# A new order of loads and products at the start of a two-block transformer kernel, and nine modulation rows moved from the attention to the projection before it

## What is computed

```python
def first_block(x, c, ...):                      # x: 512 rows of 1024
    mod = silu(c) @ w_ada + b_ada                # 3072 numbers
    shift, scale, gate = split(mod, 3)
    h = rms_norm(x, norm_pre) * (1 + scale) + shift
    proj = h @ w_in                              # 1024 -> 3072 columns
    xa, ga, q, k, v, gb = split(proj, 512 columns each)
    ya = rms_norm(rg_lru(conv(xa)) * silu(ga))   # gated linear recurrence over the rows
    yb = rms_norm(attention(rotary(q), rotary(k), v) * silu(gb))   # 8 heads of 64
    return x + gate * rms_norm(concat(ya, yb) @ w_out, norm_post)

def second_block(x, c_2, ctx_2, ...):
    mod = silu(c_2) @ w_ada_2 + b_ada_2          # 6144 numbers, and again for the context
    ...                                          # differential attention, RWKV scan, mixture of experts
```

## Time and profile before

| | us |
|---|---|
| median of 3 runs | 1869.47 |
| lowest and highest | 1867.77, 1876.37 |
| the profiled execution | 1878.58 |
| its span in the trace | 1876.8 |

### The profile page before, as it was taken

One profiled execution on the slowest core, in us unless ns is written; L12 is line 12 of the kernel. 1 busy time (PEld: TensorE's weight loads), 2 busy tenths in 40 slices (PEclk: granted clock), 3 DMA queues, 4 the chain that ended last, 5 costly groups with the idle time before them and its releaser, 6 DMA issues.

```text
span 1876.8 us, 37887 instructions
## 1 busy us (share of the span) xinstructions
PE 1717.6 (92%) x16822; PEld 927.4 (49%) x16822; DVE 804.7 (43%) x1484; ACT 518.8 (28%) x983; POOL 109.4 (6%) x144
## 2 busy tenths in 40 slices
PE   5999999999999999999999999999999977778786
PEld 3444566544546555556667667544454333323332
DVE  3853144656627456355654554344462211222210
ACT  3710254311127422354453341122231110101010
POOL 0000010010000000100000000000001101010100
PEclk8999989999989999999998998899999999999998
DMA  9121376351110030042221210356569999999997
GB/s 396 76 88 47 145 287 247 145 224 69 45 45 1 23 151 0 17 170 82 77 81 50 63 56 24 114 219 221 219 239 398 416 425 415 422 413 425 417 423 279
DMA packets 48360, 359.25 MB, mean 191 GB/s; under 512 B 8325, under 2 KB 8557, under 8 KB 28736
## 3 DMA queue, kind: packets, MB, share of 16 engines
q1 hardware_dynamic: 35792, 311.51, 41.2%
q0 software_dynamic: 12400, 45.27, 7.3%
HBM read 337.47 MB, written 27.32 MB: 194 GB/s over the span
## 4 chain that ended last, share of the span: by engine, by line
PE 74%; DMA 16%; ACT 4%; issue 3%; DVE 2%; POOL 0%; SPq 0%; ACTq 0%; DVEq 0%; POOLq 0%
PE psum L207 71%; DMA arena<-in_w 16%; PE psum L210 3%; ACT arena L204 3%; ACT L204 1%; DVE arena L154 1%; DVE arena L180 0%; DVE arena L164 0%; DVE arena L172 0%; DVE arena L160 0%; POOL arena L141 0%; DMA arena<-in_tok 0%; DVE arena L168 0%; DVE arena L159 0%; POOL out L149 0%
## 5 line engine op out<-in xcount | busy, mean ns | idle before, releaser
L207 PE MATMUL psum<-arena 32*32 32x16 f32 (+12 forms) x16178 | 1638.1, 304 | 145.2 <-DMA arena<-in_w 73.4
L207 PEld LDWEIGHTS psum<-arena 32*32 32x32 f32 (+5 forms) x16178 | 856.0, 135 | 876.3 <-issue 764.7
L204 ACT ACTIVATE arena<-psum 128x512 f32<-128x512 f32 (+5 forms) x334 | 171.4, 513 | 871.2 <-PE psum L207 670.7
L154 DVE TENSOR_TENSOR arena<-arena,psum 128x512 f32<-128x512 f32 (+3 forms) x128 | 64.9, 507 | 402.6 <-PE psum L207 209.2
L154 DVE TENSOR_TENSOR arena<-arena 128x512 f32<-128x512 f32 (+10 forms) x315 | 191.6, 608 | 31.0 <-ACT arena L204 14.7
L204 ACT ACTIVATE arena<-arena 128x512 f32<-128x512 f32 (+10 forms) x254 | 138.8, 546 | 177.7 <-DVE arena L154 41.9
L204 ACT ACTIVATE arena<-psum,arena 128x128 f32<-128x128 f32 (+3 forms) x221 | 111.7, 505 | 275.1 <-PE psum L210 135.5
L154 DVE TENSOR_TENSOR arena<-psum,arena 128x128 f32<-128x128 f32 (+3 forms) x116 | 47.4, 409 | 154.5 <-PE psum L207 141.3
L164 DVE SCALAR_TENSOR_TENSOR arena<-arena 128x512 f32<-128x512 f32 (+7 forms) x162 | 103.5, 639 | 14.5 <-ACT arena L204 8.1
L210 PE MATMUL psum<-arena 128*128 128x128 f32 x644 | 102.6, 291 | 6.1 <-ACT arena L204 3.2
L172 DVE RECIPROCAL arena<-arena 128x1 f32<-128x1 f32 (+4 forms) x71 | 79.1, 1113 | 63.0 <-ACT arena L204 59.2
(11 more groups left out here) (49 smaller groups left out, 177.7 us busy)
## 6 DMA issues: line engine op xcount, KB each, us to landing
arena<-in_w SPq DMA_DIRECT2D x127, 2048.0 KB, 34.5
arena<-in_w SPq DMA_DIRECT2D x48, 256.0 KB, 3.1
arena<-in_w SPq DMA_DIRECT2D x12, 1024.0 KB, 36.4
arena<-kd POOLq DMA_DIRECT2D x28, 256.0 KB, 3.4
gd<-arena SPq DMA_DIRECT2D x24, 256.0 KB, 3.2
arena<-gd SPq DMA_DIRECT2D x24, 256.0 KB, 5.6
arena<-in_w POOLq DMA_DIRECT2D x2, 2048.0 KB, 9.6
kd<-arena POOLq DMA_DIRECT2D x2, 1536.0 KB, 11.0
```

What stands on the lines that cost most here:

```text
L154: return self.ends(self.e.tensor_tensor(out, a, b, op))
L204: return self.ends(self.e.activation(out, a, func, **kw))
L207: return self.ends(self.e.matmul(out, lhs, rhs, start=start, stop=stop))
```

## The change

It has two parts.

**A new beginning.** The columns of the modulation matrix are reordered on the host, so that row j of the first four holds 256 columns of the shift and the same 256 of the scale: with row j alone, two of the eight k-slices of `HT` can be finished. x is loaded in four pieces, and chunk 6 in four quarters, into a buffer of its own (`EB0`, under the name `W6`), each quarter behind a modulation chunk. TensorE transposes first, then runs rows 0 and 1, and then chunk 6 a quarter at a time: two steps of k for all four tiles, whose four banks stay open, with rows 2 and 3 between the quarters. `lru_*` runs three tiles later against t than before.

**Nine rows moved.** Rows 4 to 12 are loaded one after another into `EB0` once chunk 6 is used, and each is run whole behind a tile of the first projection (t = 6, 8, ..., 22). The attention keeps rows 13 to 15, in its steps x = 0 to 8; steps 9 to 35 have none.

```diff
         def pre_sync():
...
+            for j in range(4):
+                load(j)
+                part = slice(1024 * j, 1024 * j + 1024)
+                Y.dma(EB0[:, part], T_["w"][6][:, part], d_w6[j].up("w", 6))
         def pre_tensor():
-            modulation_row(0)
             for i in range(4):
                 T.wait_ge(V["n1", i])
                 turn8("f1", i, ht1[i], ALL8)
+            modulation_row(0)
+            modulation_columns(0)
             modulation_row(1)
...
+            for j in range(4):
+                T.wait_ge(d_w6[j]["w", 6], A["ht", j], V["ht", j])
+                for m in range(4):
...
+                    for k in (2 * j, 2 * j + 1):
+                        T.mm(ps["p1", 6, m], W6[:, k, c4(m)], HT[:, k, :], k == 0, k == 7)
...
+                    elif m == 0:
+                        modulation_columns(j + 1)
+                if j < 2:
+                    modulation_row(j + 2)
...
+        ROW_AT = {2 * j - 2: j for j in range(4, 13)}
...
+                if t in ROW_AT:
+                    for q in range(3):
+                        ada_tensor(ROW_AT[t], q, ALL8)
...
-                lru_tensor(t)
+                lru_tensor(t - 3)
...
-        ADA = [(j, q) for j in range(4, 16) for q in range(3)]
+        ADA = [(j, q) for j in range(13, 16) for q in range(3)]
```

More of the change, by code:

```diff
@@ L301 @@
 XBANK = (7,)
+MODBANK = (0, 1, 2, 3)
+FIRSTBANK = (4, 5, 6, 7)
 FBANK = (0, 1)
@@ L420, in build @@
         d_fd = [dma("fd0"), dma("fd1")]
+        d_x, d_w6 = [dma(f"x{i}") for i in range(4)], [dma(f"w6{i}") for i in range(4)]
+        d_ada = dma("ada")
         d_rope, d_pw = dma("rope"), dma("pw")
@@ L640, in modulation_row @@
         def modulation_row(j):
-            T.wait_ge(V["cs"], W.landed(j), *ps.take(ALL8, "mr", j))
+            T.wait_ge(V["cs"], W.landed(j), *ps.take(MODBANK, "mr", j))
             modulation_blocks(ps["mr", j], wk(j), range(8))
@@ L672, in pre_sync @@
             Y.dma(cst, T_["consts"], d_cst.up("cst"))
-            Y.dma(X, x_in, d_x.up("x"))
-            for c in range(4):
-                load(c)
+            for i in range(4):
+                Y.dma(X[:, i, :], x_in[:, i, :], d_x[i].up("x", i))
+            for j in range(4):
+                load(j)
+                part = slice(1024 * j, 1024 * j + 1024)
+                Y.dma(EB0[:, part], T_["w"][6][:, part], d_w6[j].up("w", 6))
         def pre_tensor():
-            modulation_row(0)
             for i in range(4):
@@ L681, in pre_tensor @@
                 turn8("f1", i, ht1[i], ALL8)
+            modulation_row(0)
+            modulation_columns(0)
             modulation_row(1)
-            modulation_columns(0)
-            modulation_row(2)
-            modulation_columns(1)
-            modulation_columns(2)
-            modulation_row(3)
-            modulation_columns(3)
-        def pre_scalar():
-            def row(j):
+            for j in range(4):
+                T.wait_ge(d_w6[j]["w", 6], A["ht", j], V["ht", j])
+                for m in range(4):
+                    if j == 0:
+                        T.wait_ge(*ps.take(FIRSTBANK, "p1", 6, m))
+                    for k in (2 * j, 2 * j + 1):
+                        T.mm(ps["p1", 6, m], W6[:, k, c4(m)], HT[:, k, :], k == 0, k == 7)
+                    if j == 3:
+                        T.then_inc("p1", 6, m)
+                    elif m == 0:
+                        modulation_columns(j + 1)
+                if j < 2:
+                    modulation_row(j + 2)
+            T.mark("w", 6)
+        def pre_scalar():
+            A.wait_ge(d_par["par"])
+            A.act(sg, par[:, 0:24], ACT.Sigmoid).then_inc("cs_sg")
+            for i in range(4):
+                A.wait_ge(d_x[i]["x", i])
+                A.act(sq1, X[:, i, :], ACT.Square, accum_out=small1[:, i:i + 1])
+            A.wait_ge(V["eps"])
+            A.act(small1[:, 12:16], small1[:, 0:4], ACT.Sqrt, bias=eps[:, 0:1], scale=1.0 / D).then_inc("sq1")
+            for i in range(4):
+                turn8_act("f1", i, HT, i)
+            for j in range(4):
                 A.wait_ge(T["w", j])
@@ L869, in ada_tensor @@
             if q == 0:
-                T.wait_ge(W.landed(c), *ps.take(ring, "ada", j))
-            modulation_blocks(ps["ada", j], wk(c), ADA_K[q])
+                T.wait_ge(d_ada["w", c] if 3 < j < 13 else W.landed(c), *ps.take(ring, "ada", j))
+            modulation_blocks(ps["ada", j], W6 if 3 < j < 13 else wk(c), ADA_K[q])
             if q == 2:
@@ L892, in mods_stored @@
             return [d_mod[i % 3]["mod", i] for i in range(max(4, j - 2), j + 1)]
-        def lru_sync():
-            for j in range(4, 16):
-                load(ada_chunk(j))
         def lru_gpsimd():
@@ L1019, in att_tensor @@
                     T.then_inc("pt1", x - 2)
-                ada_tensor(*next(steps), MBANK)
+                if x < len(ADA):
+                    ada_tensor(*ADA[x], MBANK)
                 if x % 8 == 0 and x > 15:
@@ L1031, in att_tensor @@
                     T.then_inc("pv1", x - 3)
-            for step in steps:
-                ada_tensor(*step, MBANK)
         def att_gated_tensor(i):
@@ L2969, in chunks @@
     at = 0
-    parts = [(i["w_ada"][0], 8, 512), (i["w_in"][0], 8, 512), (i["w_out"][0], 8, 512), (i["w_ada_2"][0], 8, 512),
+    ada = i["w_ada"][0]
+    ada = np.concatenate([ada[:, 1024 * v + 256 * j:1024 * v + 256 * j + 256] for j in range(4) for v in range(2)] + [ada[:, 2048:]], 1)
+    parts = [(ada, 8, 512), (i["w_in"][0], 8, 512), (i["w_out"][0], 8, 512), (i["w_ada_2"][0], 8, 512),
              (w2[:, 0:3584], 8, 512), (mid, 8, 512), (w2[:, 3968:7040], 8, 128)]
```

105 lines of the change are left out of this document (46 added, 59 removed).

## The result

The changed kernel takes **1885.58 us** (median of 7 runs, 1880.46 to 1888.96), the kernel before in the same comparison 1869.47 (7 runs, 1864.18 to 1880.13). The ratio is **1.0082, interval 1.0058 to 1.0107**: slower by 0.8%. The prediction was 1869.4 with a range up to 1879.0, and 17% for slower by over 0.5%. It was wrong by 16 us and the time is outside its range. The profiled execution of the changed kernel has a span of 1887.2 us against 1876.8, so the traces have 10.4 us to explain.

What follows compares the result with a forecast made beforehand. DMA bytes were taken to bound the beginning up to 36.93 us, TensorE and its clock what follows. Terms -11.1 + 16.7 - 9.7 + 4 = -0.1 gave 1869.4 us against the median 1869.47; range 1861 to 1879.

Steps and rivals of the forecast that it cites:

- Part 1: Beginning: the first projection stands as if begun at 28.5 instead of 36.93 us, clock staying up; gain 11.1 us.
- and 5 us if DVE falls behind: First projection, tiles 5 to 8: DVE's recurrence keeps up with TensorE, taken as no cost, otherwise 5 us.
- Part 2: First projection: nine modulation rows added at 1.85 us each, nothing hiding them; cost 16.7 us.
- Part 3: Attention: 27 thirds of rows removed, worth 15.4 us, partly returned as idle time at block ends; gain 9.7 us.
- The chains at the ends of blocks: Attention: DVE passes, then ACT work, delay the copy TensorE needs; 9.5 us at first end, idle 3.2, 2.3 and 1.25.
- Part 4: Attention: first end keeps its halved stretch; one new half-clock stretch at another block end, cost 4 us.
- the sum's -0.1: Whole kernel: the beginning, added rows, removed thirds and clock together change the time by -0.1 us.
- the thin attention stays at half clock: Rival for the attention: without filler, clock falls at second block end, no recovery until the projection after; 1885 us, chance 0.1.
- it recovered at 261 with small products alone: Attention: argument against a lasting half clock, that the earlier trace's clock came back at 261 us on small products.

Runs made afterwards that it cites:

- the last version: New beginning, row 4 in the projection, other thirds put where TensorE waits in the attention, ring moved on by three, against the kernel before: 1857.71 us, ratio 0.9937.

## Why the prediction was wrong

**What bounds the kernel** was read rightly: DMA at the beginning, TensorE and its clock behind it.

**Part 1, the beginning, -11.1:** the mechanism was right, the size 10.1. The changed kernel's DMA waits are gone and chunk 1 landed at 21.91 where 22.05 was worked out. Most of the missing 1.0 is one thing. The last transposes ended at 20.2 where I had 17.5 to 18.2. The 32 take 3.66 us on a TensorE that has been at work and took 5.40 here; I had counted a cold start for row 0 and not for them. With a warm start the attention begins 0.9 us sooner. (Cold, the transposes took 5.10 to 6.67 us in different traces, so the 10.1 is good to a microsecond or so.) Apart from that, the wait for DVE that I took at nothing "and 5 us if DVE falls behind" is real without the nine rows (2.67 us in both kernels with the beginning alone) and hidden with them.

**Part 2, nine rows, +16.7:** right in kind, too low. From the beginning alone to the changed kernel the attention starts 232.92 - 217.30 = 15.6 us later, and 2.7 of DVE wait go: 18.3 us, 2.0 a row instead of 1.85. With part 1 that is +8.2 at the start of the attention, where the prediction had +5.6. The price of a row was taken from two that stand back to back. That a row between tiles of another form pays more for the change of form is my reading; it was not measured by itself.

**Part 3, thirds, -9.7:** right in kind, and too small. With the clock up the thin attention takes 73.3 us, with its waits filled, and the dense one 85.7: 12.4 us less. Part of the difference is that a thin step is shorter than worked out, 279.66 - 277.51 = 2.15 us for i = 2 in the kernel filled at the ends, where 2.28 was put. The chains at the ends of blocks are there as described: with the first end filled TensorE waits 0.83 and 2.07 us at the second, 2.9 where 2.3 was put. At the first end the chain from DVE's pass at 247.31 to the copy done at 256.79 takes 9.5 us, as worked out, but TensorE waited 1.12 and 0.58, not 3.2 in one place: thin steps brought it sooner to a wait for DVE's passes, in step 12, and behind that, at half clock, it was slower on its way to the root.

**Part 4, the clock, +4:** this is the step that failed. It says: "The first end keeps its halved stretch, about as before." The fall is there, but it came two steps earlier, at a wait of 1.12 us that the kernel before doesn't have (that it is as long as the 1.11 of before is chance), and it lasted 75 us instead of 10 and cost 23 us. In the kernel before it had cost 89.1 - 85.7 = 3.4 us, or some 4 with the dummies in the 85.7. So the term put at +4 for a new fall at another end was 23.0 - 3.4 = +19.6, from the one at the first end alone. The measured terms, -10.1 + 18.3 - 12.4 + 19.6 = 15.4, stand against the sum's -0.1; they are the +8.2 and +7.2 of the two traces taken apart. I had priced a fall by the two rows that I had, 5.1 and 2.7 us, and treated its length as a property of the fall. It isn't. In ten profiled executions, each of another kernel, TensorE had an idle time of 1.1 us or more in the attention, and half clock from there on lasted:

| kernel | idle us | steps that follow | us at 0.50 |
|---|---|---|---|
| filler in all steps | 1.11 | dense | 7 |
| before; beginning alone | 1.11; 1.10 | dense | 10 each |
| filler at later ends alone | 1.12, 0.58 | 23 us thin, then dense | 41 |
| filler from step 15 | 1.12, 1.17 | 8 us thin, then dense | 58 |
| beginning alone, ring moved on | 1.11 | dense | 99, to the end |
| filler at first end alone | 0.83, 2.07 | thin | 41, to the end |
| after; after, warm start | 1.12, 0.58; 1.13, 0.59 | thin | 75 each, to the end |
| nine rows alone | 1.50 | 24 us dense, then thin | 106, to the end |

"To the end" means to within 3 us of the last transposes of the attention. In the three kernels without such an idle time (filler at all ends, the kernel before filled, the last version) the clock never fell there. So shown is that the idle time at a block's end brings the fall, and that filling it takes the fall away, whether the other steps are thin or dense. The table also says that thin steps never brought the clock back before the end of the stage, in four traces that had only such steps from some point on. Dense ones did so after 7, 10 and 10 us, but after 18 and some 50 us where thin ones stood ahead, not in the 24 us of the nine rows alone, and once only at the end. That filler helps a recovery is what all runs say too: 1878.69 with 15 us of dummies against 1885.58, and no overlap in the ratios or the mean clocks. Which part of a thin step matters, the share of transposes or the few products, no run separates; nor the second wait, some 6 us behind the first, that comes with thin steps at the end of a block (the nine rows alone show that thin steps hold the clock down without a second wait of more than 0.28 us). **What sets the length behind dense steps stays open:** one kernel, the beginning alone with the ring moved on, ran between 1860.53 and 1909.76 us with mean clocks of 0.968 and 0.942, and no experiment here separates these runs.

Of the rivals, "the thin attention stays at half clock" had the number, 1885, and the chance 0.1. That the number fits so well is luck, since three other terms of its sum were off by 1 to 3 us each. Its mechanism was right: the clock "doesn't recover until the projection after it". It put the fall at the second end, with "some 40 us" of work behind it, which is what happened in the kernel with the first end filled. In the changed kernel it came one end earlier, and what I had missed is that the change put thin steps behind the first end as well, so that its short stretch of the earlier trace rows was no guide to it. The reason against the rival, "it recovered at 261 with small products alone", rested on one execution of a kernel in which dense steps followed. Its own price had no bound but the end of the stage, so the range should have reached up to it.

Half clock did not cost what half the speed suggests. A step of i = 3 takes 313.44 - 308.80 = 4.64 us at 0.50 against the 2.82 worked out for full clock, 1.65 times. The step of i = 2, whose 2.15 us at full clock are measured, takes 283.04 - 279.46 = 3.58, 1.67 times. By either the 75 us hold some 45 us of full-clock work, a cost of 30; 23 were measured. (The 5.1 us of Part 4 for the fall before took half clock as half speed, too; it was some 4.) The rest would be the waits at the ends, which a slower TensorE covers in part; that is argued and not measured by itself.

The Trainium skill, "TensorE: Matmul & The Clock Gate", section "A second HAM failure mode: psum-queue depth-cycling", has short idles make the clock swing. The direction agrees with the ten traces of the table. The picture doesn't: in the attention these traces show one fall and then up to 106 us without a swing back.

## What to carry to other kernels

Before filler is taken from a stage that TensorE bounds, look at where that stage waits: moved work is worth most inside waits of a microsecond or so. Here, on top of the same new beginning, the kernel was 0.8% slower than before with nine modulation rows taken out of the attention, not to be told from before with none moved (1.0006), and 0.6% faster with some of them put at a block's end. Price a fall of the clock by the work that follows, up to the next stage and beyond, and not by how long one trace held it; and look at the mean clock of every run, since two runs of one kernel here were 49 us apart, at mean clocks of 0.968 and 0.942. If an experiment changes the number of takes from a shared ring of PSUM banks, later stages get other banks: move the ring on so that they don't, or 8.68 us may turn up far away.

## What was not expected of the hardware

- After an idle time of 1.1 us the granted clock stayed at 0.50, which is 1.2 GHz, for 7 to 99 us, with TensorE busy nearly all the while: 99.00 of 99.00 us in one trace.
- Idle times of 0.36, 0.41 and 0.83 us in the attention brought no fall; 1.10 to 1.13 did at the end of the first block in each of the eight kernels that had it, in step 12 of four of them and in step 14 of the others. Its length alone doesn't decide, though: 2.67 us of waiting for DVE in the projection were followed by 3.4 us at 0.50 in one trace and by none in another.
- Eight groups of four small dummy products in one idle time made a program of 1.87 ms 0.23% faster (0.9977, 0.9956 to 0.9998), and its attention 3.4 us shorter.
- At the start of the program the clock's column reads 1.00 in every trace, but the 32 transposes took 5.10 to 6.67 us where they were TensorE's first work, and 3.66 behind 9.73 us of other products. The first record of the clock lies at 18.4 us in the trace of the changed kernel, so the 1.00 ahead of it is no measurement; a cold start shows in the durations.
